# Layer norms from sums of shifted values in a one-core hybrid encoder trunk

## The reference

```
layer 0: x <- LN_ab(ALPHA*x + mixer(x) @ w_out_ab);  x <- LN_ffn(ALPHA*x + (silu(x@w1) * (x@w3)) @ w2)
layer 1: x <- LN_c(ALPHA*x + hgrn(x) @ w_out_c);     x <- LN_moe(ALPHA*x + top-2-of-8 expert SwiGLU(x))

def layer_norm(x, g, b):
    xc = x - mean(x, -1)
    var = mean(xc * xc, -1)
    return xc * rsqrt(var + 1e-5) * g + b
```

## Time and profile before

| | |
|---|---|
| median of 3 runs | 1643.51 us (1639.65 to 1645.88) |
| profiled execution, its own time | 1643.89 us |
| its span, first to last instruction | 1642.1 us |
| PE busy | 1516.5 us (92%) |
| DVE busy | 1163.0 us (71%) |
| ACT busy | 947.4 us (58%) |
| granted TensorE clock, mean | 0.958 |

### The profile page before, as it was taken

How to read it: one execution, slowest core, us unless ns; L and a number is a source line. 1 busy time by engine, 2 the same in 40 slices (tenths; PEclk the granted TensorE clock), 3 DMA queues, 4 the chain that set the end, 5 groups by cost and what they waited for, 6 DMA issues and landing times.

```text
span 1642.1 us, 28733 instructions
## 1 busy us (share of the span) xinstructions
PE 1516.5 (92%) x11072; PEld 1357.5 (83%) x11073; DVE 1163.0 (71%) x1565; ACT 947.4 (58%) x1246; POOL 75.8 (5%) x147
## 2 busy tenths in 40 slices
PE   7889968899999899998779999999999999999992
PEld 7879967799999799998757888788888878888882
DVE  5574845555543458855369889888988988898994
ACT  4453123433332467535356787777778777777872
POOL 8200000000000000000000000000000000000000
PEclk9999987999999999988869999999999999999997
DMA  7411001244444343320559999999999999999982
GB/s 238 148 53 55 4 3 61 81 154 153 144 141 153 103 141 104 104 78 1 211 198 353 393 375 362 398 337 398 351 390 374 362 399 337 395 346 406 363 306 78
DMA packets 162029, 371.69 MB, mean 226 GB/s; under 512 B 10152, under 2 KB 85840, under 8 KB 161936
## 3 DMA queue, kind: packets, MB, share of 16 engines
q1 hardware_dynamic: 159120, 360.14, 59.8%
q0 software_dynamic: 2448, 8.91, 2.1%
q10 hardware_dynamic: 368, 1.31, 0.2%
HBM read 360.10 MB, written 10.24 MB: 226 GB/s over the span
## 4 chain that ended last, share of the span: by engine, by line
PE 77%; DVE 11%; issue 6%; ACT 4%; DMA 1%; DVEq 0%; SPq 0%; POOLq 0%; POOL 0%; ACTq 0%
PE bank L517 9%; PE bank L1061 9%; PE bank L1062 9%; PE bank L1063 9%; PE bank L519 9%; PE bank L518 9%; PE bank L601 4%; DVE w_lo L1774 4%; PE bank L1085 3%; PE bank L1087 3%; PE bank L1086 3%; PE bank L880 1%; PE bank L829 1%; PE bank L824 1%; PE bank L937 1%
## 5 line engine op out<-in xcount | busy, mean ns | idle before, releaser
L1774 DVE TENSOR_TENSOR w_lo<-moe_ring,w_hi 128x1024 fp32r<-128x1024 f32 (+1 forms) x560 | 608.3, 1157 | 43.1 <-ACT w_hi L2323 42.9
L2323 ACT ACTIVATE w_hi<-moe_ring 128x1024 fp32r<-128x1024 f32 (+1 forms) x560 | 532.5, 1014 | 86.5 <-PE bank L1087 52.9
L1135 DVE TENSOR_TENSOR wd_lo<-arena,wd_hi 128x1024 fp32r<-128x1024 f32 x142 | 171.0, 1208 | 192.5 <-ACT wd_hi L1910 192.1
L517 PE MATMUL bank<-in_hi,wd_hi 128*128 128x320 f32 x880 | 280.2, 318 | 21.7 <-DVE in_lo L1148 15.8
L1061 PE MATMUL bank<-w_hi,xe_hi 128*128 128x512 f32 (+1 forms) x768 | 289.1, 376 | 1.4 <-DVE xe_lo L1808 1.4
L1062 PE MATMUL bank<-w_hi,xe_lo 128*128 128x512 f32 (+1 forms) x768 | 287.0, 374 | 0.0
L1063 PE MATMUL bank<-w_lo,xe_hi 128*128 128x512 f32 (+1 forms) x768 | 286.4, 373 | 0.0
L518 PE MATMUL bank<-in_lo,wd_hi 128*128 128x320 f32 x880 | 276.6, 314 | 0.0
L519 PE MATMUL bank<-in_hi,wd_lo 128*128 128x320 f32 x880 | 276.4, 314 | 0.0
L1910 ACT ACTIVATE wd_hi<-arena 128x1024 fp32r<-128x1024 f32 x142 | 148.3, 1047 | 198.4 <-PE bank L519 189.7
L517 PEld LDWEIGHTS bank<-in_hi,wd_hi 128*128 128x128 f32 x880 | 169.7, 193 | 27.2 <-issue 20.8
(11 more groups left out here) (354 smaller groups left out, 1795.4 us busy)
## 6 DMA issues: line engine op xcount, KB each, us to landing
moe_ring<-in_moe_w SPq DMA_DIRECT2D x216, 1024.0 KB, 8.2
moe_ring<-in_moe_w SPq DMA_DIRECT2D x64, 768.0 KB, 4.9
arena<-in_ffn_w SPq DMA_DIRECT2D x30, 1024.0 KB, 5.2
arena<-in_w_in_c SPq DMA_DIRECT2D x16, 1024.0 KB, 5.4
arena<-in_w_in_ab SPq DMA_DIRECT2D x13, 1024.0 KB, 6.0
arena<-in_w_out_ab SPq DMA_DIRECT2D x4, 1024.0 KB, 5.3
arena<-in_w_out_c SPq DMA_DIRECT2D x4, 1024.0 KB, 5.3
arena<-in_ffn_w SPq DMA_DIRECT2D x4, 768.0 KB, 4.4
```

The lines of the kernel that those rows point to most:

```text
L517: pe.matmul(b[:, 0:T], w_[0][:, cols], x_hi, start=start, stop=False)
L1135: dve.tensor_tensor(wd_lo[:, m_ % DENSE_UNITS, 0:words], src, wd_hi[:, m_ % DENSE_UNITS, 0:words], ALU.subtract).then_inc(S("dense_lo"), 1)
L1774: dve.tensor_tensor(w_lo[:, i % UNITS, 0:unit_words(i)], moe_unit(i), w_hi[:, i % UNITS, 0:unit_words(i)], ALU.subtract)\
L2323: act.activation(w_hi[:, i % UNITS, 0:unit_words(i)], moe_unit(i), ACT.Copy).then_inc(S("e_hi"), 1)
```

## The change

1. **Early mean.** When rows 0 to 3 of `res` are there, VectorE has added them up in a new buffer `ln_acc`; after the first half of the third pair's first tile TensorE multiplies that by ones (`early_sum`), and ScalarE makes an early mean m (sum/512) in `mean`.
2. **Shift.** VectorE subtracts m from rows 0 to 3 and makes `ALPHA*x - m` for rows 4 to 7 ahead of their products, to which the PSUM bank is then added. All of `res` is thus shifted by m.
3. **Sums during the projection.** VectorE adds the shifted rows 4 to 6 in `ln_acc` and the squares 0 to 6 in `sq[:, 0]` as they come; ScalarE squares shifted rows between its roundings. (Rows 0 to 3, once shifted by their own mean, sum to zero over features.) After the last product 4 ones-matmuls remain: the two sums, row 7 and square 7.
4. **Variance** as sqs/D - (sum/D)^2: a squaring on ScalarE, one subtraction on VectorE, then logarithm and exponential.
5. **Behind it** VectorE centres by the remaining mean, scales, and makes `in_lo` from `res + b - in_hi` in one instruction (before from xT), interleaved: scale k, low part k-1, centre k+4. Each scale waits for the centrings issued so far. ScalarE makes all `in_hi` first and then all `xT`.
6. **Row by row.** The first tile of each dense_pair projection goes over k outside and the two output rows inside, so that each `in_lo[k]` gives 6 products.
7. ScalarE's rounding order: in ab the rounding of FFN_T stands behind the squares 0 to 5, in ffn that of W2_T+10 and all later ones; the second half of the tile before is behind the early mean.

```
+    def early_sum(n_):                                        # PE
+        pe.wait_ge(*at_count(n_ + "_scaled", 1))
+        b = take((n_, "early"), n_ + "_std", 1)
+        pe.matmul(b[:, 0:T], ones[:, :], ln_acc[n_], start=True, stop=True)
     def layer_norm(n_):                                       # PE
-        (8 ones-matmuls over res, 8 over sq)
+        pe.wait_ge(*at_count(n_ + "_scaled", 2))
+        pe.matmul(b[:, 0:T], ones[:, :], ln_acc[n_], start=True, stop=False)
+        pe.matmul(q[:, 0:T], ones[:, :], sq[:, 0, :], start=True, stop=False)
+        pe.wait_ge(*at_count(n_ + "_res", KC))
+        pe.matmul(b[:, 0:T], ones[:, :], res[:, KC - 1, :], start=False, stop=True)
+        pe.wait_ge(*at_count(n_ + "_sq", KC))
+        pe.matmul(q[:, 0:T], ones[:, :], sq[:, KC - 1, :], start=False, stop=True)

     def layer_norm(n_, stage):                                # DVE
+        dve.scalar_tensor_tensor(mean, sqs, 1.0 / D, ln_acc[n_], ALU.mult, ALU.subtract)
+        for k in range(EARLY_K): centre(k)
+        dve.wait_ge(*at_count(n_ + "_std", 3))
+        for k in range(KC):
+            scale(k)
+            if k > 0: rest(k - 1)
+            if k + EARLY_K < KC: centre(k + EARLY_K)
+        rest(KC - 1)

     def residual(full, n_, name, next_tiles):                 # DVE
         for j in range(KC):
             for i in next_tiles[j]: dense_rest(i)
+            if j == EARLY_K:
+                dve.wait_ge(*at_count(n_ + "_std", 1))
+                (4 x res[i] -= mean; 4 x res[i] = ALPHA*xT[i] - mean)
             dve.wait_ge(*at_count(full, j + 1))
-            res[j] = ALPHA*xT[j] + PSUM
+            (j < 4: the same; else res[j] += PSUM)
+            if first < j < KC - 1: ln_acc += res[j]            # first = 0 or 4
+            squares = {4: range(1, 3), 5: range(3, 5), 6: range(5, 7)}.get(j, ())
+            for i in squares: sq[0] += sq[i]

     def layer_norm(n_, stage):                                # ACT
-        8 squares; Ln; Exp; per k: xT, in_hi
+        ln_acc = (sum/D)^2; Ln; Exp
+        for k in range(KC): in_hi[k]
+        for k in range(KC): xT[k]

     ACT, around norm ab:
-        for i in range(OUT_T + 1, FFN_T + 1): dense_rounded(i)
+        dense_rounded(OUT_T + 1)
+        dense_rounded(OUT_T + 2)
+        half_rounded(2 * (OUT_T + 3))
+        early_mean("ab")
+        half_rounded(2 * (OUT_T + 3) + 1)
+        squares_of("ab", 0, 6)
+        dense_rounded(FFN_T)
+        squares_of("ab", 6, KC)
     ACT, around norm ffn:
+        ... half_rounded(2 * (W2_T + 7)); early_mean("ffn"); half_rounded(2 * (W2_T + 7) + 1)
+        dense_rounded(W2_T + 8); dense_rounded(W2_T + 9)
+        squares_of("ffn", 0, 6)
+        for i in range(W2_T + 10, INC_T + 1): dense_rounded(i)
+        squares_of("ffn", 6, KC)
```

More of the change, by code:

```diff
@@ L233, in mixed_trunk @@
         ff_g = tok(f_.take(2 * T), 2)
+        ln_acc = {"ab": f_.take(T), "ffn": f_.take(T)}
         res = tok(arena[:, NORM0:NORM0 + KC * T], KC)
@@ L366, in mixed_trunk @@
         shared["hgrn_sum"] = ("attention_b", 2)
[L367 to L368 removed]
+        for stage, each in (("res", KC), ("ln_full", 3), ("centered", EARLY_K), ("sq", KC), ("std", 3), ("scaled", 3 + KC), ("ln", KC)):
+            for i, n_ in enumerate(("ab", "ffn", "c")):
                 shared[n_ + "_" + stage] = ("norm_" + stage, i * each)
@@ L855, in _ @@
                             mm.then_inc(S("dense_half"), 1)
+                            if i == EARLY_K // 2 and gi == 0:
+                                early_sum("ffn")
                         elif gi < len(W2_GROUPS) - 1:
@@ L1472, in residual, with layer_norm, centre, scale @@
-            def residual(full, taken, name, next_tiles):
+            def layer_norm(n_, stage=None):
+                def centre(k):
+                    dve.scalar_tensor_tensor(res[:, k, :], where[n_, "sum"][:, 0:T], -1.0 / D, res[:, k, :], ALU.mult, ALU.add)\
+                       .then_inc(S("dve_chain"), 1)
+                    chain[0] += 1
+                def scale(k):
+                    dve.wait_ge(S("dve_chain"), chain[0])
+                    dve.scalar_tensor_tensor(res[:, k, :], res[:, k, :], vcol(f"ln_{n_}_g", k), mean[:, :], ALU.mult, ALU.mult)\
+                       .then_inc(S(n_ + "_scaled"), 1)
+                def rest(k):
+                    if stage is not None:
+                        dve.wait_ge(*at_count("in_hi", KC * stage + k + 1))
+                        dve.scalar_tensor_tensor(in_lo[:, k, :], res[:, k, :], vcol(f"ln_{n_}_b", k), in_hi[:, k, :], ALU.add, ALU.subtract)\
+                           .then_inc(S("in_lo"), 1)
+                dve.wait_ge(*at_count(n_ + "_std", 2))
+                dve.wait_ge(*at_count(n_ + "_ln_full", 3))
+                dve.scalar_tensor_tensor(mean[:, :], where[n_, "sqs"][:, 0:T], 1.0 / D, ln_acc[n_], ALU.mult, ALU.subtract)\
+                   .then_inc(S(n_ + "_scaled"), 1)
+                for k in range(EARLY_K):
+                    centre(k)
+                dve.wait_ge(*at_count(n_ + "_std", 3))
+                for k in range(KC):
+                    scale(k)
+                    if k > 0:
+                        rest(k - 1)
+                    if k + EARLY_K < KC:
+                        centre(k + EARLY_K)
+                rest(KC - 1)
@@ L1483, in _ @@
             input_rest(1, oT)
-            residual("out_ab_full", "ab_res", "out_ab", ahead(OUT_T + 1, 1, KC))
-            layer_norm("ab", "ln_ab_g")
-            input_rest(2, xT)
+            residual("out_ab_full", "ab", "out_ab", ahead(OUT_T + 1, 1, KC))
+            layer_norm("ab", 2)
             for j in range(FC):
@@ L1699, in _ @@
             output_rest(4, KC)
-            residual("out_c_full", "c_res", "out_c", ahead(OUTC_T + 1, 1, KC - 2))
-            layer_norm("c", "ln_c_g")
+            residual("out_c_full", "c", "out_c", ahead(OUTC_T + 1, 1, KC - 2))
+            layer_norm("c")
             dve.wait_ge(*at_count("c_ln", KC))
@@ L2110, in _, with early_mean @@
             act.activation(Hout.rearrange("p g f n -> p (g f n)"), where["hout", 0][:, :], ACT.Copy).then_inc(S("hout_done"), 1)
-            def layer_norm(n_, stage=None):
-                for k in range(KC):
[L2114 to L2125, removed]
+            def early_mean(n_):
+                act.wait_ge(*at_count(n_ + "_ln_full", 1))
+                act.activation(mean[:, :], where[n_, "early"][:, 0:T], ACT.Copy, scale=1.0 / (EARLY_K * P)).then_inc(S(n_ + "_std"), 1)
@@ new lines, in squares_of @@
+            def squares_of(n_, k0, k1):
+                for k in range(k0, k1):
+                    if k < EARLY_K:
+                        act.wait_ge(*at_count(n_ + "_centered", k + 1))
+                    else:
+                        act.wait_ge(*at_count(n_ + "_res", k + 1))
+                    act.activation(sq[:, k, :], res[:, k, :], ACT.Square).then_inc(S(n_ + "_sq"), 1)
+            def layer_norm(n_, stage=None):
+                act.wait_ge(*at_count(n_ + "_ln_full", 2))
+                act.activation(ln_acc[n_], where[n_, "sum"][:, 0:T], ACT.Square, scale=1.0 / D).then_inc(S(n_ + "_std"), 1)
+                act.wait_ge(*at_count(n_ + "_scaled", 3))
+                link(act.activation(mean[:, :], mean[:, :], ACT.Ln, bias=eps_norm[:, :]))
+                act.activation(mean[:, :], mean[:, :], ACT.Exp, scale=-0.5).then_inc(S(n_ + "_std"), 1)
+                if stage is not None:
+                    for k in range(KC):
+                        act.wait_ge(*at_count(n_ + "_scaled", 3 + k + 1))
+                        act.activation(in_hi[:, k, :], res[:, k, :], ACT.Identity, bias=vcol(f"ln_{n_}_b", k)).then_inc(S("in_hi"), 1)
+                for k in range(KC):
+                    act.wait_ge(*at_count(n_ + "_scaled", 3 + k + 1))
+                    act.activation(xT[:, k, :], res[:, k, :], ACT.Identity, bias=vcol(f"ln_{n_}_b", k)).then_inc(S(n_ + "_ln"), 1)
@@ L2141, in _ @@
             logs_and_exps()
-            for i in range(W2_T + 1, INC_T + 1):
+            for i in range(W2_T + 1, W2_T + 7):
                 dense_rounded(i)
+            half_rounded(2 * (W2_T + 7))
+            early_mean("ffn")
+            half_rounded(2 * (W2_T + 7) + 1)
+            dense_rounded(W2_T + 8)
+            dense_rounded(W2_T + 9)
+            squares_of("ffn", 0, 6)
+            for i in range(W2_T + 10, INC_T + 1):
+                dense_rounded(i)
+            squares_of("ffn", 6, KC)
             layer_norm("ffn", 3)
```

108 lines of the change are left out of this document (62 added, 46 removed).

## The result

| | before | after |
|---|---|---|
| median of the runs | 1643.88 us (12 runs, 1639.65 to 1645.88) | 1648.27 us (12 runs, 1641.56 to 1649.55) |
| profiled execution, own time | 1643.89 us | 1648.81 us |
| its span, mean granted clock | 1642.1 us, 0.958 | 1647.1 us, 0.948 |

What follows compares the result with a forecast made beforehand. It took TensorE, 77% of the chain, as the bound. From 1643.9 us it took 2.1 gained at unchanged clock (0.2-0.8+2.7) and added 5.2 of clock loss: 1647.0, range 1640 to 1653.

Steps and rivals of the forecast that it cites:

- The early sum: One ones-matmul inside the projection ahead of each of the three norms, adding 0.54 us on TensorE's path.
- Norm ab, the wait ahead of the sums: Behind out_ab's last product, TensorE's sums wait 3.6 us for VectorE's queue, where before they began at once.
- First product: In norm ab the first feed-forward product starts 10.6 us after the old last product's end, 4.6 us earlier.
- The second tile: Behind norm ab, its weight rounding queues behind the xT copies; it starts at 23.6 instead of 23.8 us, 0.2 gained.
- The W2 stall: Ahead of norm ffn, tile 10's first half comes 1.9 us late; the second input-projection tile starts 0.8 us later.
- Norm c: With no weights rounded behind it, the transposes, router and first gather follow 2.7 us earlier.
- The clock: Half clock after new idle gaps: 1.1 us at the sums and 1.5 at the second tile, in ab and ffn; 5.2 lost.
- Row by row: In the first tile of the other projections the new order gains 0, at most 0.3 us each.
- The rival in which the head start counts: Second tile not held behind xT, so the norms give 11.0 us together: 1633 us; chance 0.1.
- the warm clock: Gaps of 3.6 and 4.2 us on TensorE don't pull the clock down: 1641.8 us; chance 0.2.
- Cold throughout: Sums of all three norms and both second tiles at half clock: 1653.8 us; chance 0.15, shared with a longer VectorE tail.
- The change that doesn't do what it says: VectorE's tail 4 us longer, so even the first product doesn't move: 1653 us; chance 0.15, shared with cold throughout.

Runs made afterwards that it cites:

- e1: The changed kernel with ScalarE's rounding of the second tile behind norms ab and ffn moved ahead of the xT copies: 1635.04 us, ratio 0.9941.
- e4: The kernel before with the new norm only at c and first tiles row by row: 1641.49 us, ratio 0.9977.
- e3: The changed kernel with filler matmuls in TensorE's idle times ahead of the sums and of the first and second tiles: 1639.86 us, ratio 0.997.
- e7: The kernel before with the new norm only at ab and first tiles row by row: 1647.19 us, ratio 1.0019.
- e8: The kernel before with only the first tile of each projection row by row: 1643.08 us, ratio 0.9996.
- e2: The changed kernel with ffn's shifts ahead of two W2 rests, squares 4 and 5 behind the rounding of tile 10's first half: 1647.37 us, ratio 1.0008.
- e5: The changed kernel with the moves of e1 and e2 together: 1629.85 us, ratio 0.9918.
- e6: e5 with VectorE's last three additions in ab and ffn made ones-matmuls, and 7 fillers ahead of the first tile: 1627.77 us, ratio 0.9897.

## Why the prediction was right

It gave 1647.0 us, from 1640 to 1653, 0.2% slower; measured were 1648.27 and 0.24%. Against the profiled execution the forecast was +3.1 us (2.4 in ab, 3.4 in ffn, -2.7 in c), the spans differ by 5.0: 2.86, 4.52, -3.26 with the early sum of c, +1.5 in the HGRN2 stage, -0.6 in the expert stage. Its steps in turn:

- **The early sum**, 0.54 on the path: 0.70 long with an overlap, 0.54 of delay at W2's tile 9 (+2.86 to +3.40). Right.
- **Norm ab, the wait ahead of the sums.** Forecast 3.6 us behind VectorE's tail, measured 3.31 from the same instructions in the same order: shifts, additions, two rests, two square additions. Right.
- **First product.** Forecast 4.6 sooner, measured 4.36 with 0.46 of another half clock at the head of out_ab in it, so 4.8. Right.
- **The second tile** held by the xT copies: forecast 23.6 us behind the last product and 0.2 of the 4.6 left. Measured -0.2 as well (+0.26 less the 0.46). This was the step that decided, and e1 shows it by taking it away.
- **The W2 stall**, forecast 1.9, measured 1.70. But ffn without the clock came out at 1.5 us of loss rather than 0.8 (5.84 less 2.86, less 1.5 for the sums at the half clock): the wait ahead of its sums was 2.96, not 2.5, which is 0.5 of the 0.7.
- **Norm c**: 3.24 from last product to transposes by the forecast (2.7 and the early sum), 3.33 measured, and again 3.3 in e4. Right.
- **The clock, the term that was sized wrong.** Taken were 1.1 for the sums in ab and in ffn, 0 in c, and 1.5 for each second tile: 5.2. Measured were 0, 1.5 and 0 for the sums, and 2.6 and 1.54 for the second tiles: 5.6. The sum was near only since errors of both signs met. The 1.5 came from the start at 321.19 in the trace of before, a short one; its bound of 2.7, from the start at 765.55, was what ab then showed. e3, in which the clock never falls there, bears out the sum: 5.7 us of its gain arise between the last product of out_ab and the third input tile. How the sum splits is chance: in e7 the same code in ab lost 1.2 in the sums and 1.6 in the second tile, where the changed kernel lost 0 and 2.6. The prediction weighed a rule from the Trainium skill (TensorE: Matmul & The Clock Gate, HAM oscillation), that a kernel with idle gaps between bursts pays for the clock's transition at each gap. The trace of the changed kernel agrees for the gaps of 3.1 to 4.5 us ahead of the first and second tiles, all followed by half clock; it does not for the gaps of 3.31 us ahead of the sums of ab and of 1.04 ahead of those of c, after which the clock was 1.00.
- **Row by row**: forecast 0, e8 measured 0.9996.

The rival in which the head start counts (1633) failed by its own condition: FFN_T+1 was not ready before the first tile ended. e1 met that condition, and came to 1635.04. The rival with the warm clock (1641.8) failed at 315 and 329 us; made true by e3 it measured 1639.86. Cold throughout failed in ab and c, whose sums stayed at 2.4 GHz, though in e7 those of ab did fall. The change that doesn't do what it says failed at the wait ahead of the sums, 3.31 us where it needed 4 more than forecast.

Not foreseen was the HGRN2 stage, 1.5 of the 5.0 us; the norms alone gave 4.1 where the forecast was 3.1. From tile 12 of the input projection to out_c nothing is edited, and yet the profiled executions take one of three lengths, at three granted clocks. The stretch in the kernel before, in the changed one and in e1:

```profile
680.68:756.93 76.25, 73.88 (x675) 0.89 0.20 66
```

```profile
688.04:765.78 77.74, 75.38 (x675) 0.87 0.19 64
```

```profile
676.99:751.51 74.52, 72.15 (x676) 0.91 0.21 67
```

The other seven fall on the same three: 74.6 (e2), 76.2 (e3, e4, e5, e8), 77.8 (e6, e7). The kernel with the lowest median has the longest one. Length times granted clock is nearly the same in all three (67.9, 67.6 and 67.8 us), so the difference is the clock and not a wait. It is not an effect of the change in any direction that the runs show, but a step of about 1.6 us that comes and goes; why stays open. Nor does one kernel always run at the same clock: the five shorter executions of e2 had a mean granted clock of 0.951 to 0.952 over the whole kernel, the seven longer ones 0.946 to 0.947. With one profile per kernel it is a reason to read sizes from the starts around an edit, and verdicts from medians.

## What to carry to other kernels

When a stage is shortened, follow the queue of every engine up to the second piece of work behind it: what is gained at the first product is only kept if the second tile's operands come earlier by the same amount. Here one rounding behind eight copies that nobody needed yet turned a first product 4.4 us sooner in ab into nothing at the second tile, and moving it took some 11 us off the two norms (0.8% of the kernel by the medians). Work that is moved to another engine is priced where it stands in that engine's queue: three matmuls of 0.54 us were cheaper than three additions of 0.52 us, since the additions stood behind two weight rests. Where a gap on TensorE can't be closed, price the clock's fall with the whole range of such starts in the trace, and expect the same code to land elsewhere in it. And ask who paces the tile behind the gap: where VectorE does, holding the clock up gives nothing.

## What the runs showed of the hardware

- Gaps of the same length did not end alike: after 3.31 us of idle the sums of ab ran at a granted clock of 1.00 in the changed kernel; in e7, in which that part is the same code, after 3.32 us they fell to the half clock and took 3.6 us instead of 2.4. After 2.96 us those of ffn ran at 0.55 (564 to 567 us).
- A start at the half clock did not cost the same each time. A tile of 48 products takes 7.04 us at the full clock. Behind a gap it took 8.40 and 8.57 us in the kernel before (570.73, 321.19), 8.58 and 9.64 in the changed one (584.97, 330.02) and 8.65 in e7 (330.01).
- Matmuls without a purpose kept the granted clock at 1.00 across gaps of about 4 us (e3, e6). The 36 of e3, 20.5 us of TensorE's busy time, came with a kernel 8.9 us faster than the changed one, 5.7 of it in the two norms where 35 of them stand (their group: 72 records, two for each fp32 matmul).
- The first tile behind a norm took the same time at either clock: 9.58 us to the second tile at 1.00 (e6), 9.59 with most of it at 0.55 (e5), as its rows wait for in_lo.
